# A hybrid decoder trunk on one core: 14th weight slot, another slot order, norm vectors in dead memory, strided writes

## The reference, cut to what matters

```python
def reference(x, w_in, ..., w_out, ln1_g, ln1_b, router_w, router_b, exp_w_gate, exp_w_up, exp_w_down, ln2_g, ln2_b):
    for l in range(DEPTH):                                    # DEPTH = 2, x is (1, 256, 1024) float32
        proj = x @ w_in[l]
        ...                                                   # three token mixers on parts of proj
        heads_out = jnp.concatenate([o_gla, o_ssd, o_rwkv], axis=-1)
        x = layer_norm(DEEPNORM_ALPHA * x + heads_out @ w_out[l], ln1_g[l], ln1_b[l])
        ffn = grouped_moe(x, router_w, router_b, exp_w_gate[l], exp_w_up[l], exp_w_down[l])
        x = layer_norm(DEEPNORM_ALPHA * x + ffn, ln2_g[l], ln2_b[l])
    return x

def grouped_moe(x, router_w, router_b, w_gate, w_up, w_down):
    scores = jax.nn.sigmoid(h @ router_w)                     # (256, 16)
    sel = (scores + router_b).reshape(-1, 4, 4)
    ...                                                       # best group of 4, then the top 2 experts in it
    for e in range(N_EXPERTS):                                # 16 experts, 1024 -> 512 -> 1024, float32
        he = jax.nn.silu(h @ w_gate[e]) * (h @ w_up[e])
        out = out + gate[:, e:e + 1] * (he @ w_down[e])
    return out
```

## Time and profile before

| | us |
|---|---|
| median of three runs | 878.82 |
| the three runs | 875.11, 878.82, 880.15 |
| the profiled execution, its own time | 880.37 |
| its span, first to last instruction | 878.6 |
| PE busy | 829.7 (94%) |
| DVE / ACT / POOL busy | 316.8 / 181.7 / 37.2 |
| HBM read | 243.85 MB, 279 GB/s over the span |

### The profile page before, as it was taken

How to read it: one execution, slowest core, us unless ns; L and a number is a source line. 1 busy time by engine, 2 the same in 40 slices (tenths; PEclk the granted TensorE clock), 3 DMA queues, 4 the chain that set the end, 5 groups by cost and what they waited for, 6 DMA issues and landing times. The chain is left out here.

```text
span 878.6 us, 12768 instructions
## 1 busy us (share of the span) xinstructions
PE 829.7 (94%) x5343; PEld 458.2 (52%) x5343; DVE 316.8 (36%) x642; ACT 181.7 (21%) x369; POOL 37.2 (4%) x105
## 2 busy tenths in 40 slices
PE   9999999989999999999799998999799999999984
PEld 8888666455334433333388867654543343333331
DVE  1296436364112111211435945292712211111215
ACT  1142323233001120000313332241330012100001
POOL 7200000020000000000000000000200000000000
PEclk9999999989999999999999999999899999999998
DMA  9954200169899999999953522020999999899991
GB/s 277 336 191 163 97 3 17 80 244 420 350 423 420 422 399 402 422 420 420 394 190 114 192 97 98 1 97 6 408 379 366 422 422 420 339 423 421 422 418 54
DMA packets 55249, 245.83 MB, mean 280 GB/s; under 512 B 8356, under 2 KB 13328, under 8 KB 30608
## 3 DMA queue, kind: packets, MB, share of 16 engines
q1 hardware_dynamic: 53840, 240.20, 68.8%
q0 software_dynamic: 1344, 4.72, 1.5%
HBM read 243.85 MB, written 1.05 MB: 279 GB/s over the span
## 5 line engine op out<-in xcount | busy, mean ns | idle before, releaser
L548 PE MATMUL bank<-ring,xg 128*64 128x512 f32 x576 | 145.0, 596 | 4.2 <-DMA ring<-in_exp_w_up 2.2
L1045 PE MATMUL bank<-x_cm,ring 128*128 128x256 f32 x576 | 125.9, 379 | 0.9 <-ACT x_cm L2006 0.9
L1045 PEld LDWEIGHTS bank<-x_cm,ring 128*128 128x128 f32 x576 | 108.9, 190 | 16.9 <-issue 1.3
L548 PE MATMUL bank<-ring_more,xg 128*64 128x512 f32 x384 | 101.8, 596 | 1.8 <-DMA ring_more<-in_exp_w_up 1.8
L779 DVE TENSOR_TENSOR y_lo<-bank,y_hi 128x512 fp32r<-128x512 f32 x32 | 22.1, 691 | 198.6 <-issue 170.2
L548 PEld LDWEIGHTS bank<-ring,xg 128*64 128x64 f32 x576 | 44.1, 137 | 78.1 <-issue 76.4
L582 PE MATMUL bank<-ring,x_cm 128*64 128x512 f32 x336 | 78.4, 606 | 3.1 <-issue 2.0
L764 DVE TENSOR_SCALAR x_cm<-bank,g_col 128x512 f32<-128x512 f32 x32 | 24.0, 751 | 98.5 <-PE bank L548 82.1
L1052 PE MATMUL bank<-ring,x_cm 128*128 128x512 f32 x128 | 57.7, 599 | 0.0
L548 PEld LDWEIGHTS bank<-ring_more,xg 128*64 128x64 f32 x384 | 31.0, 137 | 50.5 <-issue 49.1
L710 ACT ACTIVATE y_hi<-bank 128x512 fp32r<-128x512 f32 x32 | 19.1, 597 | 176.5 <-PE bank L582 176.5
(11 more groups left out here) (383 smaller groups left out, 936.9 us busy)
## 6 DMA issues: line engine op xcount, KB each, us to landing
ring<-in_exp_w_down SPq DMA_DIRECT2D x42, 1024.0 KB, 13.6
ring<-in_exp_w_gate SPq DMA_DIRECT2D x38, 1024.0 KB, 12.7
ring<-in_exp_w_up SPq DMA_DIRECT2D x38, 1024.0 KB, 10.5
ring<-in_w_in SPq DMA_DIRECT2D x24, 1024.0 KB, 8.3
ring_more<-in_exp_w_gate SPq DMA_DIRECT2D x24, 1024.0 KB, 14.8
ring_more<-in_exp_w_up SPq DMA_DIRECT2D x24, 1024.0 KB, 13.2
ring_more<-in_exp_w_down SPq DMA_DIRECT2D x22, 1024.0 KB, 14.4
ring<-in_w_out SPq DMA_DIRECT2D x8, 1024.0 KB, 6.2
```

The source lines that it names most:

```text
L548: m = T.matmul(b[half_of(n, i), :], xg[g][:, 4 * h + k, cols], w[:, k, :], start=(h == 0 and k == 0), stop=(h == 1 and k == 3))
L1045: m = T.matmul(out_, w[:, k, c:c + n], x_cm[:, k, :], start=(k == 0), stop=(k == KD - 1))
```

## The change

- The slots: `MORE` is 6. The experts' loads take the four slots of the ring that `w_in` blocks held, then `xg[1]`, then `ring_more`, and last the four slots of `w_out`.
- The norms' vectors: `ln_vec` is gone. ln1's rows go to `x_cm` (dead after the router, in part reused by the experts later), asked for by POOL after `v_sel`; ln2's go to the first slot of `ring_more`, after its last block of the layer was read (a gate block of expert 15).
- `x_hi` and `x_lo` are walked in the order of x's rows: x is read contiguously, and the parts are written with a step of 128 elements (`by_column`).
- The router's 1 + exp is done by ACT, as a second instruction on `rt`; DVE starts with the reciprocal. One `keep_busy` matmul less stands before the selection.

```diff
-    MORE = 5
+    MORE = 6
...
-            cycle = [(at + i) % NSLOT for i in range(NSLOT)] + [NSLOT + MORE + i for i in range(ONCE)]
-            cycle += [NSLOT + i for i in range(MORE)]
+            aged = [(at + i) % NSLOT for i in range(NSLOT)]
+            cycle = aged[:4] + [NSLOT + MORE + i for i in range(ONCE)] + [NSLOT + i for i in range(MORE)] + aged[4:]
...
-        ln_vec = sb("ln_vec", [P, 2, D])
...
+        ln_rows = [x_cm[:].rearrange("p k s -> p (k s)").rearrange("p (a d) -> p a d", a=2),
+                   ring_more[:, 0].rearrange("p k n -> p (k n)").rearrange("p (a d) -> p a d", a=2)]
...
-            return row.rearrange("p (s k) -> p k s", k=KD)
+            return row.rearrange("p k s -> p s k") if len(row.shape) == 3 else row.rearrange("p (s k) -> p s k", k=KD)
...
-                            inc(G.tensor_tensor(x_lo[:, j], by_block(x_tm[:, j]), x_hi[:, j].bitcast(F32), ALU.subtract),
+                            inc(G.tensor_tensor(by_column(x_lo[:, j]), by_column(x_tm[:, j]), by_column(x_hi[:, j].bitcast(F32)), ALU.subtract),
                                 "g_xlo")
-                        pool.wait_ge(*done("v_x1", l))
-                    for i, name in enumerate(("ln1_g", "ln1_b") if which == 0 else ("ln2_g", "ln2_b")):
-                        pool.dma_start(ln_vec[:, i, :], t[name][l].partition_broadcast(P)).then_inc(ln_loaded.sem, 16)
+                        pool.wait_ge(*done("v_sel", l))
+                        for i, name in enumerate(("ln1_g", "ln1_b")):
+                            pool.dma_start(ln_rows[0][:, i, :], t[name][l].partition_broadcast(P)).then_inc(ln_loaded.sem, 16)
+                        last = max(n for n, q in enumerate(loads) if q[0] == l and slot_of[n] == NSLOT)
+                        pool.wait_ge(*done(*last_use(*loads[last][:3])))
+                        pool.wait_ge(ln_loaded.sem, 64 * l + 32)
+                        for i, name in enumerate(("ln2_g", "ln2_b")):
+                            pool.dma_start(ln_rows[1][:, i, :], t[name][l].partition_broadcast(P)).then_inc(ln_loaded.sem, 16)
...
-                keep_busy(1, 7)
+                keep_busy(1, 6)
...
-                do(recip1(score))
+                do(V.reciprocal(score, score))
...
-                    inc(A.activation(x_hi[:, j], by_block(x_tm[:, j]), ACT.Copy), "s_xhi")
+                    inc(A.activation(by_column(x_hi[:, j]), by_column(x_tm[:, j]), ACT.Copy), "s_xhi")
...
+                act.wait_ge(*done("s_route", l, 1))
+                inc(A.activation(rt[:, 1], rt[:, 1], ACT.Copy, bias=1.0), "s_route")
```

More of the change, by code:

```diff
@@ L314, in hybrid_trunk @@
                 v_sel=1, v_flag=1, g_xlo=2, v_x2=2,
-                s_x=9, s_route=1, s_first=KD, s_mu=4, s_conv=3, s_low=2, s_sq=1, s_ez=1, s_ea=1, s_g=1, s_norm=1,
+                s_x=9, s_route=2, s_first=KD, s_mu=4, s_conv=3, s_low=2, s_sq=1, s_ez=1, s_ea=1, s_g=1, s_norm=1,
                 s_e=3, s_turned=5,
@@ L368, in col, with by_column @@
             return slice(CH * i, CH * i + CH)
-        def by_block(row):
-            return row.rearrange("p (s k) -> p k s", k=KD)
+        def by_column(row):
+            return row.rearrange("p k s -> p s k") if len(row.shape) == 3 else row.rearrange("p (s k) -> p s k", k=KD)
         def by_row(h):
@@ L1573, in affine_rows @@
                     dve.wait_ge(ln_loaded.sem, 64 * l + 32 * (which + 1))
-                    do(V.tensor_tensor(x_tm[:, j], x_tm[:, j], ln_vec[:, 0], ALU.mult))
-                    inc(V.tensor_tensor(x_tm[:, j], x_tm[:, j], ln_vec[:, 1], ALU.add), "v_x1" if which == 0 else "v_x2")
+                    do(V.tensor_tensor(x_tm[:, j], x_tm[:, j], ln_rows[which][:, 0], ALU.mult))
+                    inc(V.tensor_tensor(x_tm[:, j], x_tm[:, j], ln_rows[which][:, 1], ALU.add), "v_x1" if which == 0 else "v_x2")
                 def out_half(j, hf):
@@ L1580, in out_half @@
                     do(V.scalar_tensor_tensor(out=x_tm[:, j, cs], in0=x_tm[:, j, cs] if j else bank[hf][:], scalar=bn2[:, j, 0:1],
-                                              in1=ln_vec[:, 0, cs], op0=ALU.subtract, op1=ALU.mult))
+                                              in1=ln_rows[1][:, 0, cs], op0=ALU.subtract, op1=ALU.mult))
                     ins = V.scalar_tensor_tensor(out=x_tm[:, j, cs], in0=x_tm[:, j, cs], scalar=bn2[:, j, 1:2],
-                                                 in1=ln_vec[:, 1, cs], op0=ALU.mult, op1=ALU.add)
+                                                 in1=ln_rows[1][:, 1, cs], op0=ALU.mult, op1=ALU.add)
                     ins.then_inc(out_ready, 1)
```

## The result

| | before | changed |
|---|---|---|
| median, us (20 runs each) | 880.83 | 877.88 |
| lowest to highest, us | 875.11 to 885.81 | 872.39 to 881.12 |
| profiled execution: own time / span, us | 880.37 / 878.6 | 878.77 / 877.0 |
| mean granted clock of the slowest and the fastest run of the changed kernel | | 0.971 / 0.981 |

The ratio is 0.995, with a 95% interval of 0.9931 to 0.9968: a gain of 4.4 us (2.8 to 6.1). The forecast was 6.6 us, a ratio of 0.9925, just outside the interval. The ratio compares the means; the two medians lie 2.95 us apart. The median of before, 878.82 us from three runs, became 880.83 us with 20, and the median after, 877.88 us, stands above the range of 868.8 to 876.2 us.

The account below looks back on a forecast made before the run. PE, busy 94% of the span, was taken as the limit between its waits. Slots 4.0 us plus router 1.3 us in each of two layers made 6.6 us off 878.82 us: 872.2 us, range 868.8 to 876.2 us.

Parts of the forecast that it names:

- Part 1: Expert weight slots: the 14th slot removes all PE waits for up blocks in the last experts, 4.0 us.
- That head start: Weight loads issued at 169.4 us instead of 183.2 us, behind the last transposes; claimed to buy little by itself.
- Part 2: Router: add of 1 goes to ACT; if POOL holds the bias add, this alone wins only 0.4 us.
- rival A: Router: POOL does not hold the bias add, so the gain is 9.0 us, 869.8 us; chance 0.25.
- clock arithmetic: Layer 0's router: six `keep_busy` matmuls of 0.70 us each end at 198.54 us, 0.24 us before the selection.
- Part 3: Router's strided writes: x_hi takes 1.17 us, POOL ends 0.9 us earlier; with the reciprocal's 0.4 us, 1.3 us a layer.
- rival B: Router: strided writes leave x_hi at 2.07 us, gain 0.4 us a layer, 874.0 down to 875.8 us; chance 0.18.
- The clock: Behind layer 1's selection wait: at least 1.2 us more if 1.9 us idle keeps the clock up; left out.
- Part 4: ln1's rows, requested behind the selection, land 5.0 us after issue; `v_pick` is in time, cost 0, up to 6.2 us allowed.
- Rival D: ln1's rows land late, 11.3 us from issue, delaying `v_pick`: 882.4 us, up to 885.4 us; chance 0.07.
- The sum: Whole kernel: 4.0 + 1.3 + 1.3 = 6.6 us off 878.82 us, giving 872.2 us.

## Why the prediction was right or wrong

**Part 1 held, with one step wrong.** The 4.0 us of waits went whole, and slots and vectors alone win 0.55% (0.35% to 0.74%), 4.8 us of 880.7, some of it by the clock. But "That head start by itself buys little" was read from the weights' side only. The early start is what lets the norm rows travel when DMA is free of weights; without it the kernel loses 12 us. And with 13 slots it costs: 8.8 us of waits, against 4.0 us with the old order in the kernel before.

**Part 2 held.** "No row shows a two-input DVE instruction beside POOL's x_lo" was true, and the forecast let it start as POOL ended, in effect held. That was right: rival A (869.8 us) is dead, 1.83 and 1.52 us for a 0.19 us instruction, which started beside `x_lo` and ended with it. In its clock arithmetic "six `keep_busy` matmuls" are six passes, twelve matmuls; the times are right.

The page's rule (the Trainium skill, GPSIMD Engine Reference, section 8, Key points: contention with Vector instructions in two-port mode or with two SBUF inputs) agrees with the rows of the two-input instructions; the reciprocal, one input, ran free in 0.35 us beside GpSimd. For the add of 1, one input and held for 1.92 us, the rule would need the two-port mode, which no row shows.

**Part 3 failed at its size, and with it the forecast's 1.3 us a layer.** x_hi was put at 1.17 us and measured 1.99 us; so POOL ended no 0.9 us sooner (27.5 us behind the last transposes, 27.2 us before). That is rival B at its better end, 0.4 us a layer: 0.31 and 0.61 us were seen from `t_cat` to the mask, against 1.3 us each. "I take 1.17 us, because the row shows a price of the read and none shows one of the write" chose the end of a range by which price was known, not by which was likely: for the same number of steps and bytes, the nearest row was 2.07 us. The page (the Trainium skill, SBUF — State Buffer, Specifications (TRN2), the row on cachelines), with no exception for writes, gave that answer, and the trace agrees with it.

**The clock was read in one direction only, and a loss by it was put at nothing without a reason.** It was left out as a gain of layer 1. It was never asked what a longer wait does to layer 0, where the passes had run at half clock, 4.92 us for 14 matmuls, and so filled the wait. In the profiled execution the 12 matmuls of the changed kernel ran at full clock in 2.84 us, PE waited 2.87 us in place of 0.86 us, and the clock fell: +1.5 us to the first gate matmul and 1.7 us in the dip. The forecast reckoned with 0.70 us a pass in layer 0, as if the low stretch stayed over the passes; it ended before they began. The pass that was taken away is 0.47 us of the longer wait and not enough by itself: with seven the time is the same. In the profiled spans the forecast's 6.6 us fell short by 5.0 us, of which part 3 is 1.7 us and this 3.2 us; by the medians it fell short by 3.65 us, by the means by 2.2 us. With the clock kept up by ten passes the same change gives 873.35 us. How the clock falls in one execution and not in another was not settled, so part of the exact size is luck.

**Part 4 held, on less.** ln1's rows landed 6.0 us behind their issue, against 5.0 us worked out and 6.2 us allowed, so 0.2 us of the room was left; DVE's four instructions end at 210.4 us, and `slot_gates` has no wait. The issues beside `pick` cost nothing (1.29 us for the two). Rival D did not come about, but the kernel with the old order showed its mechanism and its price.

**The sum.** In the spans, 4.0 us for the slots and 0.9 us for the routers, less 1.5 and 1.7 us of layer 0's clock, are 1.7 us, and 1.6 us were measured. The match is partly luck: it leaves out the mixers, 1.13 us faster in layer 0 and 1.74 us slower in layer 1 under low stretches that aren't tied to the change, and some 0.5 us that no stretch explains. The medians give more, 2.95 us, as the low stretches fall differently in each execution (mean clock 0.971 in the slowest and 0.981 in the fastest).

## What to carry to other kernels

When an engine is made to arrive sooner at a wait, size the filler again: behind waits of over 2 us TensorE's clock fell in 11 of 12 router stages here, and mostly fell once more in the midst of the following work; four filler passes were worth as much as the whole change. Read the clock of more than one execution, since the same kernel shows low stretches in different places. Moving an instruction off VectorE doesn't free it of GpSimd: ask which two-input instruction stands next. And where a small transfer is needed soon, start the large ones so early that they are through, rather than the small one so early that it competes.

## What the runs showed of the hardware that was not expected

- The clock dropped to 0.50 for about 3.4 us in the midst of unbroken matmuls, some 78 us after a router stage, in some layers and not in others; each cost 1.7 us.
- The low stretch ahead of the router lasted 3.4 us in one execution of the kernel with ten passes and 6.8 us in the other, which made the same 20 matmuls last 4.56 or 6.24 us.
- Behind the wait of 5.1 us at the start of layer 1 the low stretch lasted 3.4 us in some kernels and 10.2 us in others, with the same instructions there.
- ScalarE's 128x1024 copy takes 1.98 to 2.07 us whether the read or the write has the step; GpSimd's subtraction 2.84 to 2.89 us either way.
- The hold of a VectorE instruction ends with GpSimd's instruction, not with GpSimd's work: with the work cut in four, the add was free after 0.56 us, and the three instructions behind it were caught for 1.65 us.
